# Second attention: scores three heads ahead issued before a head's transposes instead of after them

## The chip, the cores and the metric

The kernel runs on one core of a Trainium2 chip. The time is the device time of one execution in microseconds, and of the kernel before it is the median of three runs.

## The reference

The program is two transformer blocks over 512 tokens of width 1024, in float32. The first block has a stick-breaking attention, a retention branch and a mixture of experts. The second block projects its input, runs two attentions of eight heads each, adds the result of an output projection, and goes on with a cross attention and a dense feed-forward layer. The change is in the two attentions of the second block, which the kernel runs as one loop over 16 heads. In short:

```python
# heads 0 to 7: latent attention over the keys that an index kept for each query
s = (q_lat @ c_sel + q_rope @ r_sel) * (D_NOPE + D_ROPE) ** -0.5
s = where(valid, s, -inf)
o = softmax(s) @ c_sel @ w_uv
# heads 8 to 15: three dilated causal patterns, merged by their log denominators
s = q @ k.T * HEAD_DIM ** -0.5, masked to each pattern
o = sum of alpha * softmax(s) @ v
```

The kernel turns both into one form: scores of 512 queries by 512 keys, only the causal part, plus a bias (0 or a large negative number for heads 0 to 7, a table for heads 8 to 15), a softmax, and a product with the values.

## The kernel before

The kernel is written engine by engine: each engine has its own list of instructions in a fixed order, and semaphores set by hand join them. Nothing reorders an engine's list. Within the stage at hand, `attend_tensor`, `attend_vector`, `attend_scalar` and `attend_gpsimd` each walk the 16 heads (`A_HEADS`).

A head's scores are causal, so query block qt (128 queries) needs 128 (qt + 1) keys. The four blocks together are 1280 columns (`SPAN`). The widest, of 512 columns, lands in one of two PSUM banks in turn (`wide_z`); the other three, 768 columns, share one area of PSUM (`rest_z`), of which there is one copy only. These steps are made for head h:

- TensorE, `scores(h)` (L1990): four matmuls in float32. The first, the wide one, waits until VectorE has read the wide block of head h - 2; the second waits until VectorE has read the other blocks of head h - 1 (`rest_read`).
- VectorE, `softmax(h, part)` (L2060 add of the bias, L2065 maximum, L2067 its negative): part 0 is the wide block, part 1 the other three. Part 0 waits for the transposes of head h - 3, as `score` has three buffers. The add sets `wide_read` or `rest_read`.
- ScalarE, `exp(h, part)` (L2102): exponentials with their sums.
- VectorE, `normalise(h)` (L2073 reciprocal, L2075 product): the wide block. GpSimd (L2139) does the other three.
- TensorE, `transposes(h)` (L2011): ten transposes of 128 x 128 into one PSUM area (`turned`), which must have been copied for the head before.
- ScalarE, `copy_t(h)` (L2112): two copies into `prob_t`.
- TensorE, `values(p)` (L2023) for the pair of heads 2p and 2p + 1; then ScalarE's `high(p)` (L2094) and VectorE's `low(p)` (L2045), which split the result for the next projection.

In its turn k an engine works on different heads:

```python
# VectorE                        # ScalarE
softmax(k + 2, 0)                # high((k - 3) // 2), k odd
normalise(k + 1)                 exp(k + 2, 0)
softmax(k + 2, 1)                copy_t(k)
low((k - 3) // 2)  # k odd       exp(k + 2, 1)
```

TensorE's turn k is `transposes(k)`, `values(k // 2 - 1)` for even k from 2 on, `scores(k + 3)`. In front of turn 0 it has issued the scores of heads 0, 1 and 2.

Of the kernel before, what the change touches and what calls it, by code (L numbers as in the profile page):

```python
# [81 lines left out]
def build(nc, d):  # L82
# [456 lines left out]
    def span(j):  # L539
        n = S - P * j  # L540
        return SEG[n], n
# [1410 lines left out]
    A_HEADS = 2 * HEADS  # L1952
# [19 lines left out]
    def attend_tensor(pe):  # L1972
        def scores(h):
            for qt in reversed(range(TB)):
                n = P * (qt + 1)
                q = slice(qt * P, (qt + 1) * P)
                if qt == TB - 1:
                    out = wide_z[h % 2]
                    if h >= 2:
                        pe.wait_ge(wide_read, h - 1)  # L1980
                else:
                    out = rest_z[:, SEG[n] - S:SEG[n] - S + n]
                    if h >= 1 and qt == TB - 2:
                        pe.wait_ge(rest_read, h)
                if h < HEADS:
                    lhs, rhs = q_a[:, h, q], k_a[:, h, 0:n]
                else:
                    r, g = HD * (h % 2), h % HEADS // 2
                    lhs, rhs = q_b[r:r + HD, g, q], k_b[r:r + HD, g, 0:n]
                mm = pe.matmul(out, lhs, rhs, start=(qt != 0), stop=True, skip_group_check=True)  # L1990
                if qt in (TB - 1, 0):
                    mm.then_inc(s_done, 1)

        def values_of_latents():
            for q in range(TB):
                pe.matmul(psum[:, 4 + q, :], c_kv[:, q * P:(q + 1) * P], w_uv[:, :, :].rearrange("p h v -> p (h v)"),
                          start=True, stop=True).then_inc(va_done, 1)

        def transposes(h):
            for ready in (s_norm, s_norm_pool):  # L2000
                pe.wait_ge(ready, h + 1)
            if h == 0:
                pe.wait_ge(va_read, TB)
            else:
                pe.wait_ge(t_read, 2 * h)
            for j in range(TB):
                o, n = span(j)
                for qt in range(j, TB):
                    src = SEG[P * (qt + 1)] + P * j
                    dst = o + P * (qt - j)  # L2010
                    mm = pe.transpose(turned[:, dst:dst + P], score[h % 3][:, src:src + P], ident[:, :])  # L2011
                if j in (0, TB - 1):
                    mm.then_inc(t_done, 1)

        def values(p):
            pe.wait_ge(t_read, 4 * p + 4)
            if p >= 1:
                pe.wait_ge(av_low, p)
            for j in range(TB):
                o, n = span(j)  # L2020
                for h in (2 * p, 2 * p + 1):
                    r, v = HD * (h % 2), v_a if h < HEADS else v_b
                    mm = pe.matmul(psum[r:r + HD, 7, S - n:S], v[:, j, (h % HEADS) * HD:(h % HEADS + 1) * HD],  # L2023
                                   prob_t[h % 3][:, o:o + n], start=(j == 0), stop=(j == TB - 1), skip_group_check=True)
            mm.then_inc(av_done, 1)
        pe.wait_ge(bank_free, FIRST_TILE["out2"] + 4)
        pe.wait_ge(ql_read, HEADS + 1)
        pe.wait_ge(fills, 6)
        rot2.wait(pe, "k_b", 1)
        scores(0)  # L2030
        values_of_latents()
        scores(1)
        scores(2)
        for k in range(A_HEADS + 1):
            if k < A_HEADS:
                transposes(k)
            if k >= 2 and k % 2 == 0:
                values(k // 2 - 1)
            if k + 3 < A_HEADS:
                scores(k + 3)  # L2040

    def attend_vector(dve):
        def low(p):
# [323 lines left out]
    with nc.Block() as block:  # L2367
# [28 lines left out]
        @block.tensor  # L2396
        def _(pe):
            project_tensor(pe)
            attend_tensor(pe)
            cross_stage_tensor(pe)  # L2400
            mlp_tensor(pe)
# [135 lines left out]
```

## Time and profile before

| | |
|---|---|
| time, median of three runs | 1790.32 us (1783.61 to 1792.76) |
| profiled execution | 1788.25 us, its span 1786.5 us |
| mean granted TensorE clock | 0.972 |
| busy over the span | TensorE 1650.9 us (92%), VectorE 900.5, ScalarE 746.2, GpSimd 662.6 |
| second attention | 1149.89 to 1239.61 us, 89.7 us, TensorE busy 80.9 |

The span runs from the first to the last instruction. PE is TensorE's matmuls, PEld its weight loads, DVE is VectorE, ACT ScalarE, POOL GpSimd. The granted clock is the share of 2.4 GHz that TensorE was given: 1.00 is 2.4 GHz and 0.50 is 1.2 GHz. A timeline row gives start, duration, engine, line, operation, output and inputs, shapes, and the count of merged instructions; what stands in brackets is how long the engine had been idle, and what ended it. In the chain, each piece was released by the one before it.

### The profile page before, as it was taken

To read this page: it belongs to the slowest core of one execution; us is meant where nothing else is said; L and a number is where in the kernel's file an instruction comes from. 1 tells how busy PE (TensorE), PEld (TensorE's weight loads), DVE (VectorE), ACT (ScalarE), POOL (GpSimd) and SP (SyncE) were. 2 spreads that over 40 slices of the span, in tenths; PEclk is the share of its full clock that TensorE was granted. 3 is DMA by queue.
4 is the path that set the end of the run, shared out by engine and by line. 5 is a ranking of instruction groups with operands and counts; after the bars stand their busy time and mean duration, and the time that the engine had idled before them with its cause. 6 is when DMAs were issued, how large, how long until landed. Compare 5 with 4: busy or idle time off the path is not lost. (4 is left out here: it accounts for less than half of the span.)

```text
span 1786.5 us, 21004 instructions
## 1 busy us (share of the span) xinstructions
PE 1650.9 (92%) x7928; PEld 1333.0 (75%) x7928; DVE 900.5 (50%) x1092; ACT 746.2 (42%) x886; POOL 662.6 (37%) x263
## 2 busy tenths in 40 slices
PE   4999999999999799999956989998998999999996
PEld 2888888578888788888845757756785788888885
DVE  4034210772464289998955568785423454141414
ACT  4244322343344487888733252376324332121211
POOL 2431264124443522333223534564440444444441
PEclk9999999999999899999978989999999999999998
DMA  4220142222226399999942222400230222322221
GB/s 158 106 72 24 59 142 96 81 71 94 94 99 262 144 421 405 391 384 387 389 178 72 87 83 81 151 8 1 102 112 23 94 71 97 115 94 95 94 94 47
DMA packets 46594, 249.23 MB, mean 140 GB/s; under 512 B 9440, under 2 KB 10208, under 8 KB 19904
## 3 DMA queue, kind: packets, MB, share of 16 engines
q1 hardware_dynamic: 40768, 237.85, 36.1%
q0 software_dynamic: 5184, 8.40, 1.3%
q10 hardware_dynamic: 576, 2.10, 0.3%
q8 instruction: 42, 0.69, 0.2%
q14 instruction: 24, 0.20, 0.0%
HBM read 238.15 MB, written 14.68 MB: 142 GB/s over the span
## 5 line engine op out<-in xcount | busy, mean ns | idle before, releaser
L148 POOL TENSOR_TENSOR w_lo<-raw,w_hi 128x2048 fp32r<-128x2048 f32 x101 | 464.8, 4602 | 740.9 <-ACT w_hi L142 740.8
L227 PE MATMUL psum<-x_hi,w_hi 128*128 128x512 f32 x872 | 346.5, 397 | 26.7 <-DVE x_lo L378 16.5
L228 PE MATMUL psum<-x_lo,w_hi 128*128 128x512 f32 x872 | 342.0, 392 | 0.0
L229 PE MATMUL psum<-x_hi,w_lo 128*128 128x512 f32 x872 | 341.9, 392 | 0.0
L142 ACT ACTIVATE w_hi<-raw 128x2048 fp32r<-128x2048 f32 x101 | 193.0, 1910 | 304.7 <-PE psum L229 304.2
L1555 DVE TENSOR_TENSOR moe_lo<-moe_w,moe_hi 128x2048 fp32r<-128x2048 f32 x99 | 225.6, 2291 | 54.0 <-ACT moe_hi L1496 53.0
L227 PEld LDWEIGHTS psum<-x_hi,w_hi 128*128 128x128 f32 x872 | 165.3, 190 | 71.5 <-DVE x_lo L378 15.4
L1496 ACT ACTIVATE moe_hi<-moe_w 128x2048 fp32r<-128x2048 f32 x99 | 189.6, 1916 | 24.0 <-PE psum L229 23.9
L229 PEld LDWEIGHTS psum<-x_hi,w_lo 128*128 128x128 f32 x872 | 165.3, 190 | 34.9
L228 PEld LDWEIGHTS psum<-x_lo,w_hi 128*128 128x128 f32 x872 | 165.8, 190 | 34.0 <-issue 0.7
L424 DVE TENSOR_TENSOR res<-res,psum 128x512 f32<-128x512 f32 x56 | 38.4, 687 | 217.6 <-PE psum L229 217.6
L227 PE MATMUL psum<-y_hi,w_hi 128*128 128x512 f32 x352 | 137.5, 391 | 0.0
L229 PE MATMUL psum<-y_hi,w_lo 128*128 128x512 f32 x352 | 137.0, 389 | 0.0
L228 PE MATMUL psum<-y_lo,w_hi 128*128 128x512 f32 x352 | 136.9, 389 | 0.0
L227 PE MATMUL psum<-moe_hi,moe_xt_hi 128*128 128x512 f32 x256 | 101.2, 395 | 0.1
L229 PE MATMUL psum<-moe_hi,moe_xt_lo 128*128 128x512 f32 x256 | 100.4, 392 | 0.0
L228 PE MATMUL psum<-moe_lo,moe_xt_hi 128*128 128x512 f32 x256 | 100.4, 392 | 0.0
L1078 POOL COPY token_col<-list_tokens 128x1 int32 (+1 forms) x20 | 19.8, 988 | 163.2 <-PE psum L1434 163.1
L227 PE MATMUL psum<-w_hi,x_hi 128*128 128x256 f32 x256 | 73.7, 288 | 3.8 <-DVE ret_v L618 2.8
L227 PEld LDWEIGHTS psum<-y_hi,w_hi 128*128 128x128 f32 x352 | 66.1, 188 | 14.0 <-issue 0.4
L228 PEld LDWEIGHTS psum<-y_lo,w_hi 128*128 128x128 f32 x352 | 66.1, 188 | 13.9 <-issue 0.2
L229 PEld LDWEIGHTS psum<-y_hi,w_lo 128*128 128x128 f32 x352 | 66.1, 188 | 13.7
(339 smaller groups left out, 2872.1 us busy)
## 6 DMA issues: line engine op xcount, KB each, us to landing
raw<-in_w_dense SPq DMA_DIRECT2D x101, 1024.0 KB, 4.8
moe_w<-in_w_moe_ahead SPq DMA_DIRECT2D x54, 1024.0 KB, 10.7
moe_w<-in_w_moe SPq DMA_DIRECT2D x48, 1024.0 KB, 9.8
yrow<-expert_rows SPq DMA_DIRECT2D x8, 512.0 KB, 10.3
res<-in_x SPq DMA_DIRECT2D x4, 512.0 KB, 5.8
decay<-in_decay SPq DMA_DIRECT2D x8, 256.0 KB, 3.8
hn_rows<-hn_tok ACTq DMA_DIRECT2D x4, 512.0 KB, 8.6
out<-res SPq DMA_DIRECT2D x4, 512.0 KB, 2.7
```

Of the source, the lines that this page charges most:

```text
L142: act.activation(w_hi[c % RING][:, :], raw[c % RING][:, :], ACT.Copy).then_inc(hi_ready, 1)
L148: pool.tensor_tensor(w_lo[c % RING][:, :], raw[c % RING][:, :], w_hi[c % RING][:, :].bitcast(F32), ALU.subtract).then_inc(lo_ready, 1)
L227: pe.matmul(out, lh, rh, start=first, stop=False)
L228: pe.matmul(out, lh, rl, start=False, stop=False)
L229: return pe.matmul(out, ll, rh, start=False, stop=last)
L424: dve.tensor_tensor(res[:, t, :], res[:, t, :], psum[:, (t0 + t) % 4, :], ALU.add).then_inc(bank_free, 1)
L1078: pool.tensor_copy(token_col[b][:, :], list_tokens[:, bass.ds(2 * n + b, 1)]).then_inc(col_done, 1)
L1496: act.activation(ring_hi[s % MOE_HI][:, :], ring[s][:, :], ACT.Copy).then_inc(moe_high, 1)
L1555: dve.tensor_tensor(ring_lo[s][:, :], ring[s][:, :], ring_hi[s % MOE_HI][:, :].bitcast(F32), ALU.subtract).then_inc(moe_low, 1)
```

## The change

TensorE's turn k issues `scores(k + 3)` first, then `transposes(k)`, then the values. The orders of VectorE, ScalarE and GpSimd stay: VectorE still has its normalising between the two parts of the maximum.

```diff
         scores(1)
         scores(2)
         for k in range(A_HEADS + 1):
+            if k + 3 < A_HEADS:
+                scores(k + 3)
             if k < A_HEADS:
                 transposes(k)
             if k >= 2 and k % 2 == 0:
                 values(k // 2 - 1)
-            if k + 3 < A_HEADS:
-                scores(k + 3)
```

## Rows read from the trace of the kernel before

**Rows 1.** The page's fourth part: lines of the chain that ended last.
```profile
PE psum L227 11%; PE psum L229 10%; PE psum L228 10%; PE psum L1990 2%; PE psum L2011 1%; PE psum L2023 1%; PE psum L2273 1%; DVE kept_bias L1880 1%; PE psum L2252 1%; DVE top L1879 1%; DVE kept_bias L1872 1%; POOL w_lo L148 1%; DVE x_lo L397 1%; ACT w_hi L142 0%; PE psum L1941 0%
```

**Rows 2.** The chain in order of time: start, us, piece; one pair of heads.
```profile
1182.36 1.28 PE psum L2011 x10
1183.64 2.30 PE psum L2023 x16
1185.95 2.35 PE psum L1990 x8
1188.30 1.09 PE psum L2011 x10
1189.39 2.41 PE psum L1990 x8
```

**Rows 3.** Windows: length, busy us (instructions) of PE, PEld, DVE, ACT, POOL; clock, DMA.
```profile
1202.80:1212.45 9.65, 9.54 (x54) 6.04 (x52) 8.94 (x22) 7.55 (x21) 6.03 (x6) 1.00 0.00 1
```

**Rows 4.** Timeline, all engines, around one head's scores and the next transposes.
```profile
1198.27 0.17 DVE L2073 RECIPROCAL sinv<-ssum 128x4 f32<-128x4 f32 x1
...
1198.53 3.02 POOL L2139 TENSOR_SCALAR score<-score,sinv 128x384 f32<-128x384 f32 x3 [1.74 <-DVE sinv L2073]
1198.87 0.95 DVE L2060 TENSOR_TENSOR score<-psum,dil_bias 128x768 f32<-128x768 f32 x1
...
1199.11 2.42 PE L1990 MATMUL psum<-k_b,q_b 64*128 64x512 f32 x8
...
1199.88 1.46 PEld L1990 LDWEIGHTS psum<-k_b,q_b 64*128 64x128 f32 x6 [0.47 <-DVE score L2060]
...
1201.65 1.28 PE L2011 MATMUL psum<-ident,score 128*128 128x128 f32 x10
1201.66 0.67 DVE L2060 TENSOR_TENSOR score<-psum,dil_bias 128x512 f32<-128x512 f32 x1
...
1203.16 0.17 DVE L2073 RECIPROCAL sinv<-ssum 128x4 f32<-128x4 f32 x1
```

**Rows 5.** Timeline: the transposes of head 12, the last with scores behind them.
```profile
1220.94 1.28 PE L2011 MATMUL psum<-ident,score 128*128 128x128 f32 x10
```

**Rows 6.** Timeline of the stage's end, behind the last scores.
```profile
1226.85 0.57 ACT L2094 ACTIVATE y_hi<-psum 128x512 fp32r<-128x512 f32 x1
...
1228.04 1.28 ACT L2112 ACTIVATE prob_t<-psum 128x512 f32<-128x512 f32 x2
...
1230.11 0.62 ACT L2102 ACTIVATE score<-score,snmax 128x384 f32<-128x384 f32 x1 [0.79 <-DVE snmax L2067]
...
1231.73 0.18 DVE L2073 RECIPROCAL sinv<-ssum 128x4 f32<-128x4 f32 x1 [1.06 <-ACT score L2102]
...
1235.12 1.28 PE L2011 MATMUL psum<-ident,score 128*128 128x128 f32 x10 [0.95 <-issue]
1235.84 1.41 ACT L2112 ACTIVATE prob_t<-psum 128x512 f32<-128x512 f32 x2 [1.03 <-PE psum L2011]
```

**Rows 7.** Timeline of the stage's start: the bias add of head 2.
```profile
1163.25 0.94 DVE L2060 TENSOR_TENSOR score<-psum,kept_bias 128x768 f32<-128x768 f32 x1
```

**Rows 8.** Timeline of TensorE alone: what ran behind three idle stretches.
```profile
1163.89 2.22 PE L2011 MATMUL psum<-ident,score 128*128 128x128 f32 x10 [3.16 <-DVE score L2075]
1165.91 3.10 PE L1990 MATMUL psum<-k_sparse,q_sparse 128*128 128x512 f32 x8
...
1230.58 1.29 PE L2011 MATMUL psum<-ident,score 128*128 128x128 f32 x10 [2.46 <-POOL score L2139]
...
1362.17 5.31 PE L2273 MATMUL psum<-cross_prob_t,v_cross 128*128 128x512 f32 x8 [2.55 <-ACT cross_prob_t L2186]
```

**Rows 9.** Windows behind those idle stretches (columns as in rows 3).
```profile
1164.00:1166.00 2.00, 2.00 (x11) 2.00 (x11) 1.43 (x5) 0.60 (x1) 2.00 (x3) 0.51 0.00 0
...
1230.00:1232.00 2.00, 1.42 (x12) 1.28 (x14) 0.90 (x4) 1.89 (x7) 0.48 (x1) 1.00 0.00 0
...
1362.00:1364.00 2.00, 1.83 (x2) 0.84 (x3) 0.67 (x1) 0.11 (x1) 0.00 (x0) 0.51 0.00 0
```

## The prediction

> **What bounds the kernel now.** I read the page first, then the chain of waits, then the stretch of the second attention by windows and by timeline. The page puts the three lines of the dense projections at the head of the chain that ended last, and TensorE's scores of this attention (L1990) right after them with 2% of the span [rows 1]. So inside this stage TensorE itself is on the chain. In order of time, the chain in the stage is an unbroken string of TensorE work: ten transposes 1.28 us, values 2.30, scores 2.35, transposes 1.09, scores 2.41, and again from the top [rows 2]. Their sum is 9.43 us, and 9.65 us passes for each two heads with the small waits; the windows show TensorE busy for 9.54 of 9.65 us, VectorE for 8.94, ScalarE for 7.55 and GpSimd for 6.03 [rows 3]. So the stage takes 4.82 us for a head, and VectorE is only 0.35 us a head behind it. The reader is to see how little slack there is: whatever puts a wait between TensorE and the others lengthens the stage.
>
> The timeline of one such pair shows where TensorE meets the others now [rows 4]. Scores begin at 1199.11, behind a head's transposes. The widest block of the scores goes to one of two banks and starts at once; the other three blocks share one area, so they wait until VectorE has added the bias to the previous head's (its 768-wide add, 1198.87 to 1199.82). TensorE goes on at 1199.88. Next come the transposes of the following head at 1201.65, just after GpSimd's normalising ended (1198.53 + 3.02 = 1201.55).
>
> **What the change does.** It adds and removes nothing: the same matmuls, vector operations and transfers run, and no DMA is issued in the loop. It moves scores(k+3) in front of transposes(k). The second part of these scores waits for the bias add of head k+2 on VectorE. Before, only values and the next transposes stood behind that wait; now transposes(k), whose input has been ready, are queued behind it. Who waits for transposes(k)?
>
> - VectorE: softmax(k+3, first part) waits for them, as the score buffer is reused.
> - ScalarE: copy_t(k) waits for them, and exp(k+2, second part) stands behind copy_t(k) on the same queue. normalise(k+2) on VectorE needs that exp, and stands in front of the bias add of head k+3. That add is what scores(k+4) wait for, and transposes(k+1) now stand behind those.
>
> This closes a ring that goes round once for each head: transposes(k), copy, exp of k+2, normalise k+2, bias add of k+3, scores k+4 (second part), transposes(k+1). Before, transposes(k+1) did not depend on the last two steps, so the ring was open. Its length from rows:
>
> 1. From the start of ten transposes to the end of both copies: 1235.12 to 1235.84 + 1.41 = 1237.25, so 2.13 us [rows 6].
> 2. The three exponentials with their sums, behind the copy, until the reciprocal that waits for them begins: 1230.11 to 1231.73, 1.62 us [rows 6].
> 3. Reciprocal to the 768-wide bias add, 1198.27 to 1198.87: 0.60; the add itself 0.95; to TensorE's next load, 1199.82 to 1199.88: 0.06 [rows 4].
> 4. Scores, second part: 768 of the head's 1280 columns. An unhindered head takes 2.35 us [rows 2], so 768/1280 of it is 1.41; the hindered one took 1.65 from 1199.88 to its end at 1201.53 [rows 4]. I take 1.50, since the wide block before it is out of the way.
>
> Sum: 2.13 + 1.62 + 0.60 + 0.95 + 0.06 + 1.50 = 6.86 us for a head, against 4.82. With 1.41 and 1.65 in step 4 it is 6.77 to 7.01. Everything else fits beneath it: values (2.30) and the wide block of the next scores (0.94) run while ScalarE and VectorE have their 3.2 us between copy and add; VectorE's first part (1.50, from 1201.66 to 1203.16 [rows 4]) runs under the copy and exponentials; GpSimd needs 3.01 of the 6.86; the conversion of the values' high part (ScalarE) and its remainder (VectorE) fall outside the ring. If any of these covers were gone, each would cost its own 0.6 to 2.3 us every second head; none is near that.
>
> **Count.** From transposes(0) at 1163.89 [rows 8] to transposes(12) at 1220.94 [rows 5] is 57.05 us now. Twelve turns of the ring are 82.3, so +25.3. At the start transposes(0) ran at 1163.89; now the second part of scores(3) comes first, and it waits for the bias add of head 2, which ended at 1163.25 + 0.94 = 1164.19 [rows 7]: transposes(0) at 1164.19 + 0.06 + 1.50 = 1165.75, +1.9. At the end no scores are left after scores(15), and the last heads are further along: from transposes(12) ScalarE works through copy (2.13) and exponentials (1.6), then the high part of the values, the first exponential and the next copy (1226.85 to 1228.04 + 1.28, 2.5 us), and exponentials again (1.6), 7.8 us; then GpSimd begins 0.3 later (1198.27 to 1198.53) and takes 3.0: transposes(15) at +11.1 us, where it stood at 1235.12 - 1220.94 = 14.2 [rows 4 to 6]. That gives back 3.1. Together +24.1 us with TensorE at full clock. What follows the stage waits for TensorE and shifts by as much; no transfer is hidden in this stage.
>
> **The clock.** TensorE now idles between the wide block and the rest of the next scores in those turns that have no values: 2.13 + 1.62 + 0.60 + 0.95 + 0.06 = 5.36 less transposes (1.25) and wide block (0.94), 3.2 us. There are seven such gaps (k = 0, 1, 3, 5, 7, 9, 11); the turns with values leave 0.9. The traces show both outcomes of such a gap: after 3.16 us idle the granted clock was 0.51 (1.2 GHz), and the ten transposes took 2.22 us instead of 1.28, the scores behind them 3.10 instead of 2.42; after 2.55 us idle it was 0.51 too, after 2.46 us it stayed at 1.00 [rows 8, 9]. So two of three, and the gaps here are longer than any of them. I take six of seven gaps at 0.94 to 1.62 us, the extra of the transposes alone and with the scores: six times 1.25 is 7.5 us. The bounds are nothing, and 1.62 in all 13 turns, 21 us.
>
> The Trainium skill, TensorE: Matmul & The Clock Gate, "What's actually happening", says that the throttled clock is the default state and activity releases it. By it these gaps are no accident and all seven would cost: 7 x 1.25 = 8.8 in place of 7.5; the gap of 2.46 us that kept its clock shows that it is not so strict.
>
> **Sum.** The profiled execution took 1788.25 us (span 1786.5). 1788.25 + 24.1 + 7.5 = 1819.9 us. The median of the runs shown is 1790.3, 2 us above it, which would make it 1822; between the two I say 1821.
>
> **The rivals.**
>
> - Ring at full clock throughout: the gaps don't lower the clock, as after 2.46 us. 1788 + 24.1 = 1812. The row behind 2.46 us speaks for it, those behind 3.16 and 2.55 us against it.
> - A shorter ring decides: if the copies and exponentials overlap with the wait more than I think, only VectorE and TensorE go round: first part 1.50, normalise 0.60, add 0.95, 0.06, scores 1.50, transposes 1.28 = 5.9 us for a head. 12 x 5.9 - 57.05 = +13.8, with +1.9 at the start 15.7, less up to 3.1: 1801 to 1804. Against it stands ScalarE's fixed order, copy before exp.
> - The clock falls in nearly every turn, with values or without: 24.1 + 21, 1833.
> - Other side, faster: if TensorE reached each scores' second part with VectorE's add already over, there would be no wait to pass on, and transposes would stop waiting for GpSimd. The idle of 3.16 us before transposes(0) [rows 8] and about 0.1 to 0.47 us per head before scores and transposes would be filled: up to 3.2 + 12 x 0.3 = 7 us, 1782. It decides if VectorE's add ends before TensorE's preceding work does. Now it ends 0.7 us after the scores' start [rows 4], and the scores are to come 1.2 us earlier; so I see little for it.
> - No change: TensorE's wait in front of the transposes is only that for GpSimd which it had anyway. It would need the ring to have slack of 2 us, which it hasn't. 1790.
>
> **Chances and range.** Ring with some gaps at low clock 0.62; ring at full clock 0.17; clock low nearly always 0.08; short ring 0.08; faster 0.02; no change 0.03. A measurement of this kernel tells about 0.5% (9 us) from no change; so faster 0.02, same 0.03, slower 0.95. The range takes in the ring with and without the clock's fall and the ends of step 4 (12 x -0.09 and 12 x +0.15, so -1 and +2): 1808 to 1832, and leaves out the short ring, the low clock throughout and the other side.
>
> **What would show it.** In the changed kernel's profile, transposes should start every 6.9 us (7.5 where the clock fell) instead of 4.8. VectorE should wait about 0.8 us for ScalarE's exp before each reciprocal. ScalarE should wait for transposes before each first copy, and never for the maximum of the second part. TensorE's busy share in the stage should drop from 0.99 to about 0.7, with granted clock below 1.00 in parts. The prediction is wrong if reciprocals wait for nothing on ScalarE (short ring), if the stage's clock is 1.00 throughout, or if the wait for the bias add is near nothing (no change).

## The result, and the profile after

The changed kernel takes 1820.39 us (median of 4 runs, 1817.39 to 1821.12) against 1789.64 us before (four runs; the 1790.32 us in the table above is the median of three of them); the ratio is 1.0173, with a 95% interval of 1.0152 to 1.0193. It is slower by 31 us. 1821 had been predicted, with 1808 to 1832 as the range.

The profiled execution has a span of 1819.3 us, 32.8 us more than before. The second attention holds all of it: from its first scores to the first matmul of the next projection it was 1149.89 to 1239.61, 89.7 us, and is now 1148.64 to 1272.07, 123.4 us. That is 33.7 more; the rest of the program took 0.9 us less in this execution. The page's fourth part, the lines of the chain that ended last, now has ScalarE and VectorE lines of this stage (L2102, L2112, L2060) that were not in [rows 1]:

```profile
PE psum L227 11%; PE psum L229 11%; PE psum L228 11%; PE psum L1990 2%; PE psum L2011 1%; ACT score L2102 1%; PE psum L2273 1%; PE psum L2252 1%; ACT prob_t L2112 1%; DVE score L2060 1%; PE psum L2023 1%; DVE kept_bias L1872 1%; POOL w_lo L148 1%; DVE x_lo L397 1%; ACT w_hi L142 0%
```

The chain in order of time shows the same in one turn. Where [rows 2] had TensorE alone, it now goes round the work of three engines, TensorE, ScalarE and VectorE (start, us, piece):

```profile
1171.26 1.56 PE psum L1990 x6
1172.83 1.11 PE psum L2011 x10
1173.96 0.81 ACT prob_t L2112
1174.77 1.47 ACT score L2102 x6
...
1176.96 0.88 DVE score L2060
1177.89 1.56 PE psum L1990 x6
```

Scores' second part, transposes, copy, exponentials, bias add, scores' second part: from 1171.26 to 1177.89 are 6.63 us, for one head. The timeline of the changed kernel has what each step waited for:

```profile
1172.66 1.26 PE L2011 MATMUL psum<-ident,score 128*128 128x128 f32 x10
1173.30 1.47 ACT L2112 ACTIVATE prob_t<-psum 128x512 f32<-128x512 f32 x2 [2.98 <-PE psum L2011]
...
1173.96 0.69 DVE L2060 TENSOR_TENSOR score<-psum,kept_bias 128x512 f32<-128x512 f32 x1 [1.43 <-PE psum L2011]
...
1176.27 0.18 DVE L2073 RECIPROCAL sinv<-ssum 128x4 f32<-128x4 f32 x1 [0.71 <-ACT score L2102]
...
1176.88 0.95 DVE L2060 TENSOR_TENSOR score<-psum,kept_bias 128x768 f32<-128x768 f32 x1
...
1177.89 1.56 PE L1990 MATMUL psum<-k_sparse,q_sparse 128*128 128x384 f32 x6 [3.11 <-DVE score L2060]
```

In this turn every engine waits for another one. In [rows 4] the waits were shorter, 0.47 us of TensorE's loads for the bias add and 1.74 us of GpSimd for the reciprocal, and none was for transposes. From 1164 to 1250 us the waits of the changed kernel add up so (waiter, releaser: us in all, times, longest):

```profile
POOL score L2139 <- DVE sinv L2073: 49.4, 11, 6.0
ACT prob_t L2112 <- PE psum L2011: 40.6, 16, 4.8
PEld psum L1990 <- DVE score L2060: 26.9, 11, 3.9
DVE score L2060 <- PE psum L2011: 25.1, 12, 3.8
PE psum L1990 <- DVE score L2060: 18.8, 8, 3.1
...
DVE sinv L2073 <- ACT score L2102: 7.8, 11, 0.7
```

The window of the whole stage (columns as in [rows 3]; it runs 1.1 us into the next projection) shows TensorE busy for 96.2 of 124.6 us at a mean granted clock of 0.88; before, it was 80.9 of 89.7 us. Without that 1.1 us it is 95.1 us. The busy time grew by 14 us with the same matmuls, which goes with the lower clock:

```profile
1148.64:1273.20 124.56, 96.20 (x429) 58.13 (x430) 74.86 (x168) 67.32 (x175) 52.70 (x49) 0.88 0.04 14
```

### The profile page after: what moved, and what is told of

Its sections match the earlier page's. It is cut to its first block and busy times, and to the rows that moved or that the text cites. A ratio compares the mean times of both kernels' runs of the same rounds, so it can differ in the third digit from the quotient of the medians.

```text
span 1819.3 us, 21004 instructions
## 1 busy us (share of the span) xinstructions
PE 1665.7 (92%) x7928; PEld 1341.9 (74%) x7928; DVE 901.3 (50%) x1092; ACT 747.5 (41%) x886; POOL 662.9 (36%) x263
```

## The experiments

Times are medians; ratios are to the kernel before on the same chip, with their 95% intervals. The median of the kernel before was 1789.6 us beside the changed kernel, 1786.9 beside experiments 1 to 4 and 1788.4 beside experiments 5 to 8, so it moved by up to 2.7 us itself; where two changed versions are compared across these groups, that belongs to the difference.

**1. Only the wide block in front.** One part of the change undone: the three blocks that wait for VectorE's bias add go back behind the transposes and values.

```diff
-            if k + 3 < A_HEADS:
-                scores(k + 3)
+            if k + 3 < A_HEADS:
+                scores(k + 3, (0,))       # wide block
             if k < A_HEADS:
                 transposes(k)
             if k >= 2 and k % 2 == 0:
                 values(k // 2 - 1)
+            if k + 3 < A_HEADS:
+                scores(k + 3, (1,))       # the other three
```

> The changed kernel with one part undone: only the wide block of scores(k+3) stands in front of transposes(k); the other three blocks, which wait for VectorE's bias add, stand behind the transposes and the values again. Theory (the ring closes because transposes(k) are queued behind that wait): the ring is open and the time is that of the kernel before, 1786 to 1791 us, transposes every 4.8 us. Rival A (issuing scores ahead costs in itself, by whatever it does to TensorE's order): most of the 31 us stay, over 1810 us. Rival B (the wide block in front helps, since VectorE gets it 1.2 us sooner): 1783 us.

Measured: 1786.62 us, ratio 0.9998 (0.9984 to 1.0011). The whole loss is gone, so it came from the three blocks' place in front of the transposes, and not from issuing scores ahead as such: rival A falls. The timeline of TensorE in this kernel shows a turn whose wait for the bias add (0.95 us here) has only the scores behind it:

```profile
1202.87 1.31 PE L2011 MATMUL psum<-ident,score 128*128 128x128 f32 x10
...
1205.13 1.88 PE L1990 MATMUL psum<-k_b,q_b 64*128 64x384 f32 x8 [0.95 <-DVE score L2062]
...
1206.94 1.31 PE L2011 MATMUL psum<-ident,score 128*128 128x128 f32 x10
```

Two heads take 9.42 us (1202.87 to the same place at 1212.29) instead of 9.65. Rival B's gain is thus in the trace, but it is 0.23 us for a pair (the whole stage took 88.0 us against 89.7 in the profiled executions) and under what the runs can tell.

**2. ScalarE out of the ring.** In the changed kernel:

```diff
             if k + 2 < A_HEADS:
                 exp(k + 2, 0)
-            if k < A_HEADS:
-                copy_t(k)
             if k + 2 < A_HEADS:
                 exp(k + 2, 1)
+            if k < A_HEADS:
+                copy_t(k)
```

> The changed kernel, with ScalarE's exponentials of the second part (head k+2) in front of its copies (head k). Theory: the ring goes through ScalarE (copy, then exp); with exp first it is the shorter one of VectorE and TensorE, 5.9 us for a head instead of 6.7 at full clock, the idle gaps shrink from 3.1 to 2.3 us and the clock falls less often: 12 x 0.8 = 10 us less at least, 1802 to 1810 us; VectorE's reciprocal no longer waits for ScalarE. Rival (ScalarE is not in the ring, only VectorE's own work and TensorE are): 1820 us, no change.

Measured: 1815.51 us, ratio 1.0152 (1.0123 to 1.0181), 5 us under the changed kernel (4 by the ratios, whose intervals overlap) where 10 or more were expected. The timeline of TensorE shows two turns, one behind a low clock and one at full clock:

```profile
1204.41 2.37 PE L1990 MATMUL psum<-k_b,q_b 64*128 64x384 f32 x6 [2.11 <-DVE score L2060]
1206.72 2.39 PE L2011 MATMUL psum<-ident,score 128*128 128x128 f32 x10
1209.04 3.74 PE L2023 MATMUL psum<-prob_t,v_a 128*64 128x512 f32 x16
1212.71 2.42 PE L1990 MATMUL psum<-k_b,q_b 64*128 64x512 f32 x8
1215.06 1.31 PE L2011 MATMUL psum<-ident,score 128*128 128x128 f32 x10
1216.30 1.12 PE L1990 MATMUL psum<-k_b,q_b 64*128 64x512 f32 x2
1219.54 1.56 PE L1990 MATMUL psum<-k_b,q_b 64*128 64x384 f32 x6 [2.11 <-DVE score L2060]
1221.03 1.31 PE L2011 MATMUL psum<-ident,score 128*128 128x128 f32 x10
```

At full clock a turn is 5.97 us (1215.06 to 1221.03), the 5.9 that was expected, and no reciprocal waits for ScalarE there. But behind another gap of the same 2.11 us the clock fell, the scores, transposes and values took 2.37, 2.39 and 3.74 us instead of 1.56, 1.31 and 2.37, and that turn took 8.34 us (1206.72 to 1215.06). The theory of the ring holds: from transposes(0) to transposes(12) it is 79.7 us where the changed kernel has 89.2, the 10 us less that were expected. What the expectation lacked is the end of the stage. With the exponentials in front, the last copies wait for them, and transposes(14) wait for a copy:

```profile
1256.78 2.37 PE L2011 MATMUL psum<-ident,score 128*128 128x128 f32 x10 [3.82 <-ACT prob_t L2112]
1259.07 4.32 PE L2023 MATMUL psum<-prob_t,v_b 128*64 128x512 f32 x16
```

The clock fell behind this gap too. From transposes(12) to (15) it is 16.3 us here and 12.7 in the changed kernel, so 3.6 of the 9.5 us are lost again. My guess that shorter gaps would keep the clock does not hold either; experiment 7 tests what the clock costs here.

**3. Normalising out of the ring.** In the changed kernel:

```diff
             if k + 2 < A_HEADS:
                 softmax(k + 2, 0)
-            if k + 1 < A_HEADS:
-                normalise(k + 1)
             if k + 2 < A_HEADS:
                 softmax(k + 2, 1)
+            if k + 1 < A_HEADS:
+                normalise(k + 1)
```

> The changed kernel, with VectorE's normalise(k+1) behind both parts of the maximum of head k+2 instead of between them. Theory: the bias add that scores wait for no longer stands behind normalise, which waits for ScalarE's exp; the ring is then first part 1.50, add 0.95, scores 1.45, transposes 1.28 and 0.15 between, 5.3 us for a head; gaps of about 1.6 us keep the clock: 12 x 5.3 against 12 x 4.75, plus 2 at the start, 1794 to 1800 us. Rival (ScalarE's copies, or GpSimd's normalising that now starts later, keep the ring at 6.7): over 1812 us.

Measured: 1804.04 us, ratio 1.0082 (1.0066 to 1.0099). The rival falls (over 1812), and the result is 4 us above the upper end of the theory's range. The timeline of TensorE:

```profile
1174.29 1.56 PE L1990 MATMUL psum<-k_sparse,q_sparse 128*128 128x384 f32 x6 [1.70 <-DVE score L2060]
1175.69 1.25 PE L2011 MATMUL psum<-ident,score 128*128 128x128 f32 x10
1176.88 2.37 PE L2023 MATMUL psum<-prob_t,v_a 128*64 128x512 f32 x16
1179.18 2.42 PE L1990 MATMUL psum<-k_sparse,q_sparse 128*128 128x512 f32 x8
1181.44 1.25 PE L2011 MATMUL psum<-ident,score 128*128 128x128 f32 x10
```

A turn without values is the ring of 5.2 us (transposes at 1170.48 and 1175.69). A turn with values is 5.75 (1175.69 to 1181.44), without any wait: there TensorE's own work, 1.1 + 2.3 + 2.35, is longer than the ring. Before the change a long turn and a short one made up for each other, 9.65 us for two. With transposes behind a wait in every turn they can't, and each turn costs the longer of the two. I had reckoned the ring for all twelve. The expectation also had gaps of about 1.6 us keep the clock. Later in this kernel it fell, behind a wait of 1.52 us:

```profile
1196.38 2.35 PE L1990 MATMUL psum<-k_b,q_b 64*128 64x384 f32 x6 [1.52 <-DVE score L2060]
1198.67 2.39 PE L2011 MATMUL psum<-ident,score 128*128 128x128 f32 x10
```

**4. Matmuls in the gaps.** The changed kernel with work for TensorE whose result nothing uses:

```diff
+                    if qt == TB - 2 and h in (3, 4, 5, 7, 9, 11, 13, 15):
+                        pe.wait_ge(va_read, TB)
+                        if h >= 7:
+                            pe.wait_ge(av_low, (h - 5) // 2)
+                        for _ in range(6):
+                            pe.matmul(psum[:, 7, 0:256], ident[:, :], k_b[:, 0, 0:256],
+                                      start=True, stop=True, skip_group_check=True)
```

Measured: 1812.46 us, ratio 1.0144 (1.0127 to 1.0161), as the theory had it. The window of its stage has the clock at 1.00:

```profile
1148.91:1261.34 112.43, 102.83 (x520) 66.34 (x520) 74.42 (x167) 66.43 (x173) 52.60 (x49) 1.00 0.05 16
```

Its turns are 6.62 to 6.78 us throughout. So the stage's 33.7 us are two things in these two profiled executions: 112.4 - 89.7 = 22.7 us for the ring, and 123.4 - 112.4 = 11.0 us for the clock. The 89.7 us hold one fall of the clock themselves, in front of transposes(0), which cost 0.94 + 0.68 = 1.6 us [rows 8]; at full clock on both sides the ring would be about 24 us (an estimate). Over all runs the clock's part is less sure: 7.9 us by the medians, and 5 us by the ratios (1.0173 and 1.0144), whose intervals just overlap.

**5. The same edit of VectorE on the kernel before.** The diff is that of experiment 3, with transposes in front of scores.

> The kernel before (transposes in front of scores), with VectorE's normalise(k+1) behind both parts of the maximum. It is the control for the same edit on the changed kernel, which brought that from 1820 to 1804 us. Theory: with the ring open, this edit takes no wait away, as TensorE waits under 0.5 us for the bias add; it delays the reciprocal by the add and the maxima (0.95 + 1.25 = 2.2 us), so GpSimd's normalising ends later and transposes, which now start 0.1 us after it, wait: 2 us in the turns where that was close, every second one, 1798 to 1808 us. Rival (GpSimd has slack, since it idles 1.8 us in each turn): 1786 to 1792 us.

Measured: 1813.0 us, ratio 1.0142 (1.0120 to 1.0163). The direction and the mechanism were right, the size was not. The timeline of this kernel:

```profile
1196.71 0.17 DVE L2073 RECIPROCAL sinv<-ssum 128x4 f32<-128x4 f32 x1
...
1196.97 3.02 POOL L2139 TENSOR_SCALAR score<-score,sinv 128x384 f32<-128x384 f32 x3 [5.55 <-DVE sinv L2073]
...
1200.09 2.12 PE L2011 MATMUL psum<-ident,score 128*128 128x128 f32 x10 [2.43 <-issue]
...
1202.13 3.17 PE L2023 MATMUL psum<-prob_t,v_a 128*64 128x512 f32 x16
```

The reciprocal comes after the maxima, GpSimd ends at 1199.99, and transposes begin 0.1 us later, after 2.4 us of idle TensorE. Here too the clock fell behind that gap (2.12 and 3.17 us instead of 1.28 and 2.30), in each pair of heads, 1.7 us a pair, and that is what the expectation lacked in the loop. It lacked the end of the stage as well: from transposes(12) to (15) it is 19.2 us here against 14.2. So one edit of VectorE's order takes 16 us from the changed kernel and adds 25 to the one before.

**6. Half of the turns.** Scores in front in turns 0 to 5, behind from turn 6 on.

```diff
-            if k + 3 < A_HEADS:
+            if k < 6:
                 scores(k + 3)
...
+            if 6 <= k and k + 3 < A_HEADS:
+                scores(k + 3)
```

> The change in turns 0 to 5 alone; from turn 6 on transposes stand in front of scores again. Theory (each changed turn costs its own length of the ring, and a low clock follows some gaps): 6 x 1.9 = 11 us, 2 at the start, 1 to 3 for the clock: 1800 to 1804 us, about half of the whole change. Rival (one late start is enough and the rest of the loss follows from it): near 1820 us. Rival (the loss comes from the last heads only): 1787 us.

Measured: 1801.48 us, ratio 1.0084 (1.0061 to 1.0107), about half of the whole by the ratios (13 of 31 us by the medians). The five turns from transposes(0) to (5) take 35.8 us, as in the changed kernel (36.0). From transposes(6) on, the heads have their old distances (1204.10, 1209.97, 1213.74: 9.64 us for two). The cost is paid turn by turn.

**7. ScalarE out of the ring, and matmuls in the gaps.** The edit of experiment 2 and that of 4, with four unused matmuls in place of six.

> The changed kernel, with ScalarE's exponentials in front of its copies and with four of the unused matmuls in the same gaps (the gaps are shorter here). Alone, the order of ScalarE brought the turn to 5.97 us at full clock, yet the time fell by 5 us only, and the fillers alone brought 8 us. Theory (the low clock took back what the shorter ring gave): with both, every turn is about 6.0 us at full clock, 12 x 0.7 = 8 to 9 us below the fillers alone: 1802 to 1806 us. Rival (the shorter turns of ScalarE's order were an accident of single turns): 1809 to 1813 us.

Measured: 1805.41 us, ratio 1.0104 (1.0082 to 1.0125). Its first four turns are 5.83 us and the other eight 5.91 to 5.97, so the rival falls. Against experiment 4 it is 7 us less: in the profiled executions its twelve turns take 71.0 us against 80.6, 9.6 less, and its end, transposes(12) to (15), takes 15.2 us against 11.6, 3.6 more. Against experiment 2 it is 10 us less (9 by the ratios), and the twelve turns are 8.7 us shorter (71.0 against 79.7). That is what the low clock cost in experiment 2, as much as the 8.6 us (89.2 against 80.6) that it cost in the changed kernel's twelve turns. So the low clock had not hidden the shorter ring, which shows in full with it and without; the longer end had hidden part of it.

**8. A version of its own.** Experiment 1 with unused matmuls in its two remaining gaps.

```diff
+            if k == 0:
+                pe.wait_ge(va_read, TB)
+                filler(psum[:, 7, 0:256], 5)
             if k < A_HEADS:
                 transposes(k)
+            if k == 13:
+                pe.wait_ge(wide_read, 15)
+                filler(psum[:, 0, 0:256], 5)
```

> The kernel with only the wide block in front of the transposes, and five unused matmuls in each of the two idle stretches of TensorE that it has left (in front of transposes(0), and behind transposes(13)). In its profile the clock fell behind both, which made ten transposes take 2.4 and 2.1 us instead of 1.3. Theory: 1 to 2 us less in all, 1784 to 1786 us, at the edge of what can be measured. Rival: no gain, 1787 us.

Measured: 1785.51 us, ratio 0.9985 (0.9974 to 0.9996), 12 runs. The interval lies below 1, by little. Transposes(0) ran in 1.28 us, and so did the transposes behind the other filler; the stage took 86.2 us in the profiled execution. It has the lowest ratio of all kernels here, 0.15% under the kernel before, but its interval overlaps that of experiment 1. The same matmuls in the kernel before were not tried.

## Why the prediction was right

**The ring.** The step that carried the forecast, transposes(k) behind a wait that depends on transposes(k - 1), is shown by experiments 1 and 6, and its members by 2 and 3: with ScalarE's copy and exponentials out, 5.97 us; with normalising out, 5.2. The predicted 6.86 us for a turn measured 6.63 in heads of the first kind and 6.77 in the others, at full clock. The terms: transposes to the end of the copies 2.11 (2.13 predicted); exponentials to the reciprocal 1.50 (1.62, since ScalarE begins them 0.1 us before the copy's record ends); reciprocal to the add's end 1.56 (1.55); scores' second part 1.40 and 1.49 (1.50). What was to fit beneath the ring did at full clock.

**The start and the end.** Transposes(0) begin 17.1 us after the stage's first scores, where it was 14.0; at full clock (experiment 4) it is 15.8, so +1.8 of ring, as forecast (1.9). At the end, 3.1 us were to come back: from transposes(12) to (15) it is now 12.7 us against 14.2, so 1.5, and 11.6 at full clock, so 2.6. The twelve turns between were to add 25.3 us and add 23.6 at full clock (80.6 against 57.05). The sum at full clock was forecast as 24.1 us and measured as 22.7.

**The clock** is the term that was mis-sized most: 7.5 us forecast, 11.0 measured in the profiled executions (5 to 8 over all runs, as said under experiment 4). The count of falls was right in sum, not in place. The timeline of TensorE in the changed kernel has gaps of equal length with either outcome:

```profile
1171.26 1.56 PE L1990 MATMUL psum<-k_sparse,q_sparse 128*128 128x384 f32 x6 [3.11 <-DVE score L2060]
...
1177.89 1.56 PE L1990 MATMUL psum<-k_sparse,q_sparse 128*128 128x384 f32 x6 [3.11 <-DVE score L2060]
...
1191.13 2.93 PE L1990 MATMUL psum<-k_sparse,q_sparse 128*128 128x384 f32 x6 [3.11 <-DVE score L2060]
1193.86 2.34 PE L2011 MATMUL psum<-ident,score 128*128 128x128 f32 x10
```

Counted as in the prediction, by the transposes in front of them, the gaps behind transposes(0) and (1) kept 1.00; those behind (3), (5), (7), (9) and (11), and one of 2.65 us in front of transposes(0), were followed by 0.50. That is five of the seven gaps and one at the start, which the prediction had not counted as a gap, six falls in all. The price of one was on average 11.0/6 = 1.8 us, not 1.25. My rows ended the low clock inside the next scores; in the changed kernel it lasted through the values as well, as the chain shows (from scores' second part on, TensorE alone):

```profile
1206.94 2.57 PE psum L1990 x6
1209.51 2.33 PE psum L2011 x10
1211.84 3.47 PE psum L2023 x16
1215.31 2.35 PE psum L1990 x8
```

The values took 3.47 us instead of 2.30, and then the next scores came late for the ring, too. TensorE's own work set the pace until transposes at 1217.59, a turn of 8.15 us. The low clock thus cost twice, once in the ring and once in a turn that values filled. The terms of ring and clock erred by 1.4 us too much and 3.5 too little; they cancelled in part, and the stage came out 2.1 us above their sum. That the whole came within 1 us of the forecast (1820.4 against 1821) is partly luck: besides these two errors, the rest of the program took 0.9 us less in the profiled execution, and the figure of 1821 was chosen between two bases. The mechanism was not luck, as each member of the ring was taken out or timed.

**The rule from the skill** (the Trainium skill, TensorE: Matmul & The Clock Gate, "What's actually happening": the low clock is the default, activity releases it) fits experiment 4, where unused matmuls alone kept the granted clock at 1.00 and took 11.0 us from the stage. That all gaps would cost, as I read it, is not so: two of seven gaps of 3 us kept their clock.

**The rivals.** The ring at full clock throughout is experiment 4, and not this kernel. The short ring does exist, but only with ScalarE's order changed. The clock low in nearly every turn would have been 1833 us; there were six falls, and seven of the twelve turns were lengthened by 0.8 us or more. The faster side and no change are ruled out by the measured ratio. The signs that I named in advance are there: reciprocals wait 0.71 us for ScalarE (0.8 forecast), ScalarE waits for transposes and in none of the waits from 1164 to 1250 us for the maximum's second part, transposes come every 6.6 to 7.0 us in five turns and every 7.6 to 8.3 in the seven that a fall lengthened. TensorE's busy share is 0.77 where I said 0.7, since a low clock makes it busier.

## What to carry to other kernels

Before moving an instruction forward in an engine's list, look at what it waits for, and then at who waits for what now stands behind it: if the two are joined, on however many engines, a ring closes, and each turn costs its whole length, or the longest engine's own work where that is more (experiment 3). The wait itself (0.47 us here) says nothing of that length (6.6 us). Move only the part that waits for nothing new: the wide block here cost nothing when moved alone, and gained nothing that the runs can tell. And test an engine's order together with those of its partners, and look at the end of the loop as well as at a turn (experiments 2 and 5 lost 3.6 and 5 us there): VectorE's normalising between the two maxima is 25 us better with transposes in front, and 16 us worse with scores in front.

## What the runs showed of the hardware that was not expected

- TensorE's clock fell behind gaps as short as 1.52 us (experiment 3) and 2.11 us (experiment 2), and stayed at 2.4 GHz behind gaps of 3.11 us in the changed kernel. The length of one gap does not tell which it will be; what does was not tested.
- Matmuls whose result is thrown away made this kernel faster, by 8 us as the medians have it (1820.4 to 1812.5) and 5 us by the ratios, as they kept the clock at 1.00 where it had been 0.88 in the stage.
